# Moving two thirds of an adaLN modulation into the first tile of the prompt's attention

## The reference

```python
mod = (jax.nn.silu(c) @ w_mod + b_mod)[:, None, :]
sh1, sc1, gt1, sh2, sc2, gt2 = jnp.split(mod, 6, axis=-1)
h = x * (1 + sc1) + sh1
x = LN1(DN_ALPHA * x + (1 + gt1) * token_mixer(h, ...))
h = x * (1 + sc2) + sh2
x = LN2(DN_ALPHA * x + (1 + gt2) * peer(h, ...))
```

## Time and profile before

| | us |
|---|---|
| median of 3 runs | 4479.56 |
| lowest and highest | 4474.02, 4484.35 |
| the profiled execution, its own time | 4486.73 |
| its span in the trace | 4484.9 |
| modulation (to the projection's first load) | 0 to 101.5 |
| projection of the prompt (to the attention's first load) | 101.5 to 180.8 |
| attention of the prompt (to the retrieval's first load) | 180.8 to 356.2 |

### The profile page before, as it was taken

How to read it: one execution, slowest core, us unless ns; L and a number is a source line. 1 busy time by engine, 2 the same in 40 slices (tenths; PEclk the granted TensorE clock), 3 DMA queues, 4 the chain that set the end, 5 groups by cost and what they waited for, 6 DMA issues and landing times. The chain is left out here.

```text
span 4484.9 us, 36769 instructions
## 1 busy us (share of the span) xinstructions
PE 3565.6 (80%) x10274; PEld 1778.4 (40%) x10274; DVE 3057.9 (68%) x7027; ACT 794.3 (18%) x1597; POOL 2663.2 (59%) x2632
## 2 busy tenths in 40 slices
PE   8875588487777775588888888888888888888877
PEld 1444344254454543334333333343333333333333
DVE  1126755577777786877777777777777777777774
ACT  0231110144444443101111111111111111101100
POOL 0000134455555554577777777777777777777775
PEclk9778799778888887799999999999999999999999
DMA  8320567697777776999999999999999999999998
GB/s 324 110 112 24 181 221 247 240 329 266 258 262 258 258 253 239 342 419 416 413 420 416 414 416 414 413 414 412 411 419 417 413 420 413 411 420 416 412 412 325
DMA packets 436080, 1500.23 MB, mean 335 GB/s; under 512 B 47316, under 2 KB 67796, under 8 KB 433620
## 3 DMA queue, kind: packets, MB, share of 16 engines
q0 software_dynamic: 368640, 1342.34, 76.4%
q1 hardware_dynamic: 51928, 128.60, 7.7%
q10 hardware_dynamic: 15360, 27.53, 1.6%
HBM read 1464.96 MB, written 33.33 MB: 334 GB/s over the span
## 5 line engine op out<-in xcount | busy, mean ns | idle before, releaser
L1677 PE MATMUL e_acc<-e_up,e_diag 128*128 128x512 f32 x4096 | 1948.0, 621 | 334.0 <-DMA e_up<-in_up,e_idx 229.0
L1580 DVE CUSTOM_DVE_ANT_0 e_down<-e_down,e_h_ps 128x1024 f32<-128x1024 f32 x1024 | 1244.6, 1220 | 664.9 <-DMA e_down<-in_down,e_idx 663.1
L1677 PEld LDWEIGHTS e_acc<-e_up,e_diag 128*128 128x128 f32 x4096 | 760.1, 195 | 1481.7 <-issue 813.1
L1507 POOL DMA_INDIRECT e_down<-in_down,e_idx x1024 | 996.5, 973 | 354.6 <-issue 235.1
L1507 POOL DMA_INDIRECT e_up<-in_up,e_idx x1024 | 1003.5, 980 | 328.0 <-issue 271.7
L272 POOL DMA_INDIRECT w_in_a<-in_up,a_idx_up x192 | 223.6, 1165 | 273.8 <-DVE sums L303 212.9
L544 PE MATMUL p_acc<-w_in_a,p_h1t 128*128 128x512 f32 x640 | 296.6, 624 | 45.8 <-DVEq L465 45.7
L1050 PE MATMUL a_turn<-ident_sb,a_prob 128*128 128x128 f32 x784 | 152.3, 337 | 174.9 <-ACT a_prob_t L794 168.4
L303 DVE SCALAR_TENSOR_TENSOR sums<-w_in_a,a_wgt,sums 128x1024 f32<-128x1024 f32 x192 | 263.4, 1372 | 31.8 <-DMA w_in_a<-in_up,a_idx_up 25.3
L1220 ACT ACTIVATE e_gate_e<-e_best,e_neg_b 128x16 f32<-128x16 f32 x64 | 19.7, 307 | 1462.0 <-DVEq L1273 1462.0
L264 POOL DMA_INDIRECT w_in_a<-in_down,a_idx_down x192 | 227.1, 1183 | 78.2 <-issue 50.3
(11 more groups left out here) (206 smaller groups left out, 3541.4 us busy)
## 6 DMA issues: line engine op xcount, KB each, us to landing
wm<-in_w_mod SPq DMA_DIRECT2D x12, 2048.0 KB, 9.4
w_in_a<-in_w_in SPq DMA_DIRECT2D x4, 4096.0 KB, 18.9
e_down<-in_down,e_idx POOLq DMA_INDIRECT x1024, 9.4
e_up<-in_up,e_idx POOLq DMA_INDIRECT x1024, 9.4
w_in_a<-in_w_query SPq DMA_DIRECT2D x1, 8192.0 KB, 29.2
p_xt<-in_x_t SPq DMA_DIRECT2D x10, 512.0 KB, 3.1
scratch_qt<-p_qk_t ACTq DMA_DIRECT2D x10, 512.0 KB, 3.1
a_q_t<-scratch_qt SPq DMA_DIRECT2D x20, 256.0 KB, 6.4
```

The source lines that it names most:

```text
L1507: pool.indirect_dma_start(ring, None, table, bass.IndirectOffsetOnAxis(ap=index, axis=0)).then_inc(landed, 16)
L1580: nc.vector.tensor_tensor_reduce(row, row, h2_ps[:], 1.0, 0.0, ALU.mult, ALU.add, dots[n % 2][:, s:s + 1]).then_inc(dotted, 1)
L1677: mm = nc.tensor.matmul(acc[t % 2][:, c * 512:(c + 1) * 512], diag[n % 2][:, s, :], up[:, r % RING, c * 512:(c + 1) * 512], start=n % PH = ...
```

## The change

Modulation keeps the four slices of shift1 and scale1, with a buffer for each, and stores no rows. w_in is loaded right behind the slices and the zero stores come after it. The 1 of the scales and gates is now added with the bias, in one instruction a slice.

The other eight slices are loaded in the prompt's attention into four column blocks of `w_in_a`: four behind v_a, the other four behind w_out, each when the slice that lay in its block has been multiplied. In the first tile PE multiplies half a slice (four matmuls) at the end of every head's step, into an unused half of the scores' banks. DVE adds bias and 1 in steps 2, 4, ... 14 of the first tile and in step 0 of the second. SP stores gate1, shift2 and scale2 (three of the four vectors of `mod_rows`) when the last mask of the first tile is done and six slices are added, waits for the store, and loads `rows` from it; so DVE's wait for these constants moves from step 8 of the first tile to step 3 of the second. gate2 is stored after the eighth slice, and only then is w_query loaded into `w_in_a`. The diff, without declarations of semaphores and buffers:

```diff
+MOD_CH = 512
+MOD_FIRST, MOD_REST = 2 * D // MOD_CH, 4 * D // MOD_CH
...
-    CH, BUFS = 512, 4
-    NCH = 6 * D // CH
+    CH = MOD_CH
+    NCH = MOD_FIRST
...
-            sp.dma_start(bias[:], io["b_mod"].partition_broadcast(2)).then_inc(small_in, 16)
-            for b in range(BUFS):
+            sp.dma_start(bias[:], io["b_mod"][0:2 * D].partition_broadcast(2)).then_inc(small_in, 16)
+            for b in range(NCH):
                 sp.dma_start(wm[b][:], w_mod[:, :, b * CH:(b + 1) * CH]).then_inc(w_in_sem[b], 16)
-            with sp.Fori(1, NCH // BUFS) as r:
-                for b in range(BUFS):
-
-                    sp.wait_ge(row_done, (r - 1) * BUFS + b + 1)
-                    hold(sp)
-                    sp.dma_start(wm[b][:], w_mod[:, :, bass.ds((r * BUFS + b) * CH, CH)]).then_inc(
-                        w_in_sem[b], 16)
+            w_in = io["w_in"].rearrange("(c p) n -> p c n", p=P)
+            sp.dma_start(keep["w_in_a"][:, :, 0:VA], w_in[:, :, 0:VA]).then_inc(keep["w_in_first"], 16)
+            sp.dma_start(keep["w_in_a"][:, :, VA:], w_in[:, :, VA:2048]).then_inc(keep["w_in_loaded"], 16)
+            sp.dma_start(keep["w_in_b"][:], w_in[:, :, 2048:INW]).then_inc(keep["w_in_loaded"], 16)
+
             sp.wait_ge(zeroed, 1)
             for slot in (0, 3, 4, 13):
                 sp.dma_start(io["kb"][slot], zeros[:]).then_inc(stored, 16)
                 sp.dma_start(io["vb"][slot], zeros[:]).then_inc(stored, 16)
-
-            w_in = io["w_in"].rearrange("(c p) n -> p c n", p=P)
-            sp.dma_start(keep["w_in_a"][:, :, 0:VA], w_in[:, :, 0:VA]).then_inc(keep["w_in_first"], 16)
-            sp.dma_start(keep["w_in_a"][:, :, VA:], w_in[:, :, VA:2048]).then_inc(keep["w_in_loaded"], 16)
-            sp.dma_start(keep["w_in_b"][:], w_in[:, :, 2048:INW]).then_inc(keep["w_in_loaded"], 16)
-
-            sp.wait_ge(mod_ready, 1)
-            sp.dma_start(io["mod_rows"], mod[:, 2 * D:6 * D]).then_inc(stored, 16)
-            sp.wait_ge(stored, 16 * 9)
+            sp.wait_ge(stored, 16 * 8)
...
-            with dve.Fori(0, NCH // 2) as r:
-                for b in range(2):
-                    j = r * 2 + b
-                    dve.wait_ge(row_done, j + 1)
-                    nc.vector.tensor_tensor(mod[:, bass.ds(j * CH, CH)], rows[b][0:2, :],
-                                            bias[:, bass.ds(j * CH, CH)], ALU.add).then_inc(row_copied, 1)
+            for j in range(NCH):
+                dve.wait_ge(row_done, j + 1)
+                nc.vector.scalar_tensor_tensor(out=mod[:, j * CH:(j + 1) * CH], in0=rows[j % 2][0:2, :],
+                                               scalar=1.0 if j >= NCH // 2 else 0.0,
+                                               in1=bias[:, j * CH:(j + 1) * CH], op0=ALU.add, op1=ALU.add
+                                               ).then_inc(row_copied, 1)
             dve.wait_ge(row_copied, 2 + NCH)
-            chain(nc.vector.tensor_scalar(mod[:, D:3 * D], mod[:, D:3 * D], 1.0, None, ALU.add))
-            chain.then(nc.vector.tensor_scalar(mod[:, 4 * D:6 * D], mod[:, 4 * D:6 * D], 1.0, None, ALU.add))
...
-            with pe.Fori(0, NCH // BUFS) as r:
-                for b in range(BUFS):
-                    pe.wait_ge(w_in_sem[b], (r + 1) * 16)
-                    pe.wait_ge(row_copied, r * BUFS + b + 1)
-                    for c in range(DC):
-                        mm = nc.tensor.matmul(rows[b % 2][0:2, :], silu[:, 2 * c:2 * c + 2], wm[b][:, c, :],
-                                              start=(c == 0), stop=(c == DC - 1))
-                    mm.then_inc(row_done, 1)
+            for b in range(NCH):
+                pe.wait_ge(w_in_sem[b], 16)
+                pe.wait_ge(row_copied, b + 1)
+                for c in range(DC):
+                    mm = nc.tensor.matmul(rows[b % 2][0:2, :], silu[:, 2 * c:2 * c + 2], wm[b][:, c, :],
+                                          start=(c == 0), stop=(c == DC - 1))
+                mm.then_inc(row_done, 1)
...
+            mod = sb("mod", [2, 4 * D])
+            wm = [keep["w_in_a"][:, :, b * MOD_CH:(b + 1) * MOD_CH] for b in range(4)]
...
+            rows_ps = [score[b][0:2, 512:1024] for b in range(2)]
+            bias_in, wm_in = keep["mod_small"], keep["mod_w"]
+            row_done, row_added, mod_stored = keep["mod_row_done"], keep["mod_row_copied"], keep["mod_stored"]
+            ROWS, SMALL, STORES = MOD_FIRST, 32, 16 * 8
...
+
+            def load_rows():
+                rows_dram = io["mod_rows"][seq:seq + 1, 0:3 * D].rearrange("a n -> (a n)")
+                sp.dma_start(rows[:].rearrange("p a d -> p (a d)"), rows_dram.partition_broadcast(P)
+                             ).then_inc(const_in, 16)
+
+            def load_mod(n):
+                lo = (MOD_FIRST + n) * MOD_CH
+                sp.dma_start(wm[n % 4], io["w_mod"].rearrange("(c p) n -> p c n", p=P)[:, :, lo:lo + MOD_CH]
+                             ).then_inc(wm_in[n % 4], 16)
...
                 if not first:
                     wait(masked, i * HEADS + 2)
                 sp.dma_start(mask_a[:], io["mask_a"][i][:, 0:S]).then_inc(maska_in, 16)
+                if not first and not side:
+                    wait(row_added, 2 + ROWS + MOD_REST * 3 // 4)
+                    sp.dma_start(io["mod_rows"][:, 0:3 * D], mod[:, 0:3 * D]).then_inc(mod_stored, 16)
+                    sp.wait_ge(mod_stored, STORES + 16)
+                    load_rows()
                 if not first:
                     wait(x2_ready, i)
                     sp.dma_start(x_in, io["x"][t - 1]).then_inc(x_sem, 16)
                     return
-                rows_dram = io["mod_rows"][seq:seq + 1, 0:3 * D].rearrange("a n -> (a n)")
                 sp.dma_start(v_a[:], io["va"][seq].rearrange("n p c -> p n c")).then_inc(kv_in, 16)
-                sp.dma_start(rows[:].rearrange("p a d -> p (a d)"), rows_dram.partition_broadcast(P)
-                             ).then_inc(const_in, 16)
+                if side:
+                    load_rows()
+                else:
+                    sp.dma_start(mod[:], io["b_mod"][2 * D:6 * D].partition_broadcast(2)).then_inc(bias_in, 16)
+                    for n in range(4):
+                        load_mod(n)
                 for j in range(2):
                     sp.dma_start(ln[:, j, :], io["ln1"][j].partition_broadcast(P)).then_inc(const_in, 16)
                 if not side:
                     sp.dma_start(gn[:], io["gn"]).then_inc(keep["w_out_loaded"], 16)
                     sp.dma_start(keep["w_out"][:], io["w_out"].rearrange("(c p) n -> p c n", p=P)
                                  ).then_inc(keep["w_out_loaded"], 16)
+                    for n in range(4, MOD_REST):
+                        sp.wait_ge(row_done, ROWS + n - 3)
+                        load_mod(n)
 
             tiled(sp, load)
             if not side:
 
                 sp.dma_start(keep["keys"][:], io["keys_t"]).then_inc(keep["w_query_loaded"], 16)
+                sp.wait_ge(row_done, ROWS + MOD_REST)
+                sp.wait_ge(row_added, 2 + ROWS + MOD_REST)
+                sp.dma_start(io["mod_rows"][:, 3 * D:4 * D], mod[:, 3 * D:4 * D]).then_inc(mod_stored, 16)
+                sp.wait_ge(mod_stored, STORES + 32)
                 sp.dma_start(keep["w_in_a"][:], io["w_query"].rearrange("(c p) n -> p c n", p=P)
                              ).then_inc(keep["w_query_loaded"], 16)
...
+            def add_bias(n):
+
+                at = slice(n * MOD_CH, (n + 1) * MOD_CH)
+                dve.wait_ge(bias_in, SMALL + 16)
+                dve.wait_ge(row_done, ROWS + n + 1)
+                nc.vector.scalar_tensor_tensor(out=mod[:, at], in0=rows_ps[n % 2],
+                                               scalar=0.0 if D <= n * MOD_CH < 2 * D else 1.0,
+                                               in1=mod[:, at], op0=ALU.add, op1=ALU.add).then_inc(row_added, 1)
+
             def body(i, first, last):
                 for h in range(HEADS):
                     mask(i, h)
+                    if not side and first and h >= 2 and h % 2 == 0:
+                        add_bias(h // 2 - 1)
+                    if not side and not first and h == 0:
+                        add_bias(MOD_REST - 1)
+                    if not side and not first and h == MIX_AT[0]:
+                        dve.wait_ge(const_in, CONSTS)
                     if not first and h == M_AT:
                         merge(i - 1)
                     if not first and h == READ_AT:
                         mix(i - 1)
                     if not (first and h < 1):
                         denominator(*before(i, h, 1))
-                    if first and h == 8:
+                    if side and first and h == 8:
                         dve.wait_ge(const_in, CONSTS)
...
+            def modulate(n, half):
+
+                pe.wait_ge(wm_in[n % 4], n // 4 * 16 + 32)
+                if n >= 2:
+                    pe.wait_ge(row_added, 2 + ROWS + n - 1)
```

(33 more changed lines are left out.)

## The result

| | before | after |
|---|---|---|
| median | 4481.95 us (4 runs) | 4533.96 us (4 runs) |
| lowest and highest | 4474.02, 4488.95 | 4523.24, 4534.48 |
| profiled execution: own time, span in the trace | 4486.73, 4484.9 | 4523.24, 4521.4 |

The ratio is 1.0117 with a 95% interval of 1.0091 to 1.0143: the kernel became 52 us **slower**, where 0.26% faster was forecast.

What follows compares the result with a forecast made beforehand. Modulation was taken as bound by TensorE, its end by the DMA queue, and the first attention tile by TensorE at half clock. Terms -49.7 + 5.4 + 54.9 + 1.4 - 22.8 - 1 = -11.8 gave 4467.8 us, range 4460 to 4484.

Steps and rivals of the forecast that it cites:

- the low clock: Rival: TensorE stays at 1.2 GHz in the first attention tile, +65 us in all, 4545 us; chance 0.13.
- Modulation, four slices: End of modulation: the next stage's first load is issued at 51.8 instead of 101.50, -49.7 us.
- the wait for slice 0: First attention tile, head 0: TensorE waits until slice 0 lands behind v_a, +5.4 us (4 to 9.4).
- matmuls: First attention tile: 64 added matmuls are 128 records of 0.43 us at 2.4 GHz, +54.9 us.
- slow start: First attention tile: the first added records run slower after the wait, as at modulation's start, +1.4 us.
- what the clock gives back: First attention tile: added matmuls raise TensorE to 2.4 GHz, so its own 47.2 us become 24.4, -22.8 us.
- Second tile: Second attention tile: its chain begins with scores of 0.91 instead of 1.65 us, -1 us (0 to -3).
- side case of 380 GB/s throughout: Modulation: if the queue ran at 380 GB/s throughout, the gain would be -47 us.
- Later slices: Prompt's attention: slices after slice 0 land before they are needed, 8 us of cover at slice 4; costs nothing.
- Modulation rows: SP's queue, end of first attention tile: storing and reloading gate and shift rows costs nothing, up to 5 us if late.

Runs made afterwards that it cites:

- e1: The changed kernel with 192 unused bytes per partition added behind `silu`; 4474.45 us, ratio 0.9983 to the kernel before.
- e3: The changed kernel with 192 unused bytes per partition added behind `w_in_a`; 4467.32 us, ratio 0.9981 to the kernel before.

## Why the prediction was wrong

**The step that failed** stands in its first paragraph: "a microsecond off an early stage comes off the end, unless a later stage waits for something that the early one used to deliver". The sum ends with the prompt's attention and takes every later stage to keep its time. The change had a part that no term priced: a tile that now lives through the program, and with it a new address for all that is allocated behind it. (The diff ahead of the prediction leaves out the declarations, and there it stands.) No rival covered it either; the one on the other side, the low clock, did not happen. A tile of the experts took 337.0 us instead of 329.0: 8 us in each of seven tiles and 5.5 behind them are 62 us against a gain of 5.

The steps before that, against the trace of after:

| step | forecast | measured | from |
|---|---|---|---|
| "Modulation, four slices" | -49.7 | -49.8 | 51.69 against 101.50 |
| the wait for slice 0 (part of the next row) | +5.4 | +6.4 | the idle time at 148.25 |
| the first tile: wait, matmuls, slow start and "what the clock gives back" | +38.9 | +43.4 | v_a to the last scores: 97.23 against 238.48 - 184.62 |
| "Second tile" | -1 | +1.5 | those scores to r_h2t: 119.19 against 117.71 |
| sum | -11.8 | -4.9 | 351.31 against 356.19 |

- *Modulation* came out to 0.1 us. (Its side case of 380 GB/s throughout gives -48 by its own bytes, and not -47; nothing rests on it.)
- *The clock* was right: 1.00 through the tile, and two stationary columns were enough. This term could have cost 77 us, and the argument from the second tile and from modulation carried it.
- *The first tile* was mis-sized by 4.5 us: 1.0 in the wait, and 0.19 in each of the 16 heads. A banded head takes 5.52 us where 1.90 and four matmuls of 0.86 make 5.33, a dilated one 4.97 where 2.62 x 1.90/3.68 and the same matmuls make 4.78. Half of that stood in the earlier trace rows: eight such records take 264.12 - 260.60 = 3.52 there and 164.61 - 161.08 = 3.53 here, where the sum took 3.43 for them. The rest of the 4.5 is the slow start: the first eight records took 5.40 instead of 3.43 us, 2.0 and not 1.4 more.
- *The second tile* had the wrong sign. ScalarE's work between the tiles (copies, squares, and two table loads) takes as long at either clock of TensorE: 6.2 us from its copy of the heads to its copy of the next probabilities, before and after. The wait of TensorE for that copy in the kernel before (timeline of PE), and the timeline of ACT in the kernel after:

```profile
249.23 0.87 PE L1050 MATMUL a_turn<-ident_sb,a_prob 128*128 128x128 f32 x3 [2.16 <-ACT a_prob_t L794]
```

```profile
237.82 1.28 ACT L844 ACT_TABLE_LOAD   x1
...
239.43 1.28 ACT L854 ACT_TABLE_LOAD   x1
...
241.53 0.46 ACT L816 COPY a_prob_t<-a_turn 128x384 f32<-128x384 f32 x1
```

  At 1.2 GHz TensorE waited 2.16 us for that copy; at 2.4 GHz it is there earlier and waits 4.86, and in 238 to 250 its clock is 0.61 in the mean. The wait takes back what the faster heads gained, and the scores and the output projection behind it, at the low clock again, cost the rest.
- *Later slices* and *Modulation rows* at nothing: right. There is no second wait of TensorE for a slice, and the retrieval's r_h2t comes 4.9 us earlier although w_query is issued at 236.51 as before.

Without the shift the forecast's kernel exists: e1 and e3 are at 0.9983 and 0.9981, 8 us faster by the ratios (5 and 12 by the medians), close to the 11.8 that were put down, and just under what was called the least that can be told. How close is in part luck: up to the retrieval their profiles are 4.8 and 4.9 us ahead, as that of the kernel after is.

What stays open: the stretch from the retrieval to the first y took between 1505 and 1533 us in the fourteen profiles, with the kernel before at 1529 and the kernel after at 1509, and follows none of the edits. It is most of why single times differ by 20 us, and part of the 52 us can be scatter of this kind.

## What to carry to other kernels

A new tile that outlives its stage is part of the change: list which buffers move, and see where the large transfers of the *other* stages now land, above all in the stage that takes the most time. Here the experts fill three fifths of the span, and a pad of 192 bytes a partition was worth 60 us. An operand's address can be tested alone in one run, by a pad in the kernel before, with no instruction changed.

## What the runs showed of the hardware

- A gather of 4 KB rows into SBUF slots that start 64 or 128 bytes off a multiple of 256 moves 404 to 405 instead of 414 GB/s and lands in 11.4 to 11.7 instead of 9.4 us. Half of the gathers off costs 0.5 to 1.2 us of 329 a tile here; by its rows POOL, which issues one each 1.285 us, holds the tile there.
- The DMA share reads 1.02 in both kernels, at 329 us a tile and at 337, and doesn't tell the two limits apart; POOL's waits for a free slot (18.2 against 64.3 us) do.
- In the first attention tile the same scores and sums ran at 0.50 while TensorE was busy in 5.00 of 5.00 us, and at 1.00 with eight records of 512 columns a head between them.
